# Two edits in a two-layer decoder kernel: the mLSTM gates loaded chunk by chunk, and the compressor's input kept in its own order

## The chip, the cores and the metric
The kernel runs on one core of a Trainium2 chip. The metric is the device time of one execution in microseconds (us); less is better. The inputs are fixed, all data is float32, and the whole program is one launch.

## The reference, cut to what matters
One inference step of a two-layer trunk, for a prompt of 1024 tokens and a sample group of 8 x 8 tokens. Layer 0 has mLSTM heads (4 heads, keys of 64, values of 128) beside gated DeltaNet heads. Layer 1 has NSA heads, one of whose branches attends to compressed blocks, beside FoX heads. The two places that the change touches compute this:

```python
# mLSTM, for each chunk of tokens, after the chunkwise recurrence gave num and den:
#   h = num / max(|den|, bound);  h = rmsnorm(h) * mi_norm;  out = h * sigmoid(output gate)
# NSA compression: overlapping blocks of 32 tokens, stride 16, of keys (kv = 0) and values (kv = 1):
#   unit  = the 16 tokens x 64 numbers of one stride, flattened
#   block = two units in a row + position embedding, flattened to 2048
#   out   = silu(block @ cmp_w1) @ cmp_w2          # 2048 -> 256 -> 64
```

## The kernel before, in words
The program is a row of stages. Each stage has its own instruction lists for TensorE (PE), ScalarE (ACT), VectorE (DVE), GpSimd (POOL) and the DMA queue of SyncE (SP). Each list runs in the order written. A wait in a list (`need`, `wait_ge`) holds up all that stands behind it in that list. At the end of a stage all engines meet at a barrier, so a stage lasts as long as its longest chain. A float32 matmul of the code is two matmul instructions in the trace (64 in the code of L2319 are 128 in the trace); data marked with `r32` is one pass.

**The stage `mlstm`.** The tokens are handled in nine chunks: the sample group (called NC, index k = 0), then the prompt chunks i = 0 to 7 of 128 tokens (index k = i + 1). For chunk i, PE prepares chunk i + 1 (`prepare`: row broadcasts, transposes, scores ST, L542 to L558), reads out chunk i (`read_out`, L580, L582), and updates the state (`update`, L592). DVE adds masks (`decay`, L752), multiplies weights, moves the numerator out of PSUM (`out`, L792 to L799, with a `tensor_scalar` at L795) and updates the state (L780). ACT takes exponentials (L648), and sums of squares of a chunk (L666).

The end of each chunk is done later, as a chain of steps for each index k: `scaled(k)` on DVE (L822) multiplies by a factor; `turn_back(k)` on PE (L612) transposes four heads into the one PSUM bank HT; `gated(k)` on DVE (L829) multiplies by the gate into Z; `high(k)` on ACT (L676) rounds; `low(k)` on POOL (L724) subtracts. `turn_back(k)` waits for `gated(k - 1)`, since there is one HT bank. The factors come from `factors(n)` on DVE (L805 to L815), for a batch of chunks at a time, with a square root on ACT (L671) in its middle. The square root needs another activation table than the exponential.

Before, there are three batches: k = 0 to 4 (factors at i = 3), k = 5, 6 (factors at i = 5), k = 7, 8 (factors behind the loop). The chunk ends are handled as this table says; 7 and 8 come behind the loop:

```python
    batches = (slice(0, 5), slice(5, 7), slice(7, 9))
    finished = {4: (0, 1), 5: (2, 3), 6: (4,), 7: (5, 6)}
```

The gates (sigmoid already taken, in DRAM as `G`) are loaded by one DMA (L503) for all tokens, and multiplied by mi_norm on POOL (L720, four instructions of 128 x 1092) before the first `low`.

**The stage `tables`.** Twelve groups of 256 tokens (four of the prompt, eight of the sample group's pages) come in through four slots (L2192, L2198). PE turns each (L2252) so that numbers lie in the partitions. ACT copies a group from PSUM into X with two instructions, one for keys and one for values (L2367). X has, in each partition, 8 runs (a = 0 to 7) of 386 numbers: run a holds the number of each unit n at place a. The compressor is the loop at L2319: 4 kinds (keys or values, two halves of the hidden size) of 16 matmuls, each with 385 moving columns, which lie side by side in X. Behind each kind DVE copies one column (L2422) and ACT applies silu (L2371). The last two columns hold the position embedding, loaded by four DMAs of ACT's queue (L2350).

**Elsewhere.** One line outside of both stages is used as a yardstick, at L1206 in the stage `delta`:

```python
            step("VT", A.activation(VT, V.rearrange("p s t -> p t s"), ACT.Copy))
```

It copies 128 x 1024 numbers from SBUF to SBUF. It writes them side by side and reads them with a step of 32 numbers. L398 copies as many from SBUF to SBUF, side by side on both sides; L404 half as many. In `stream`, L236 is the matmul with `r32` data.

Of the kernel before, what the change touches and what calls it, by code (L numbers as in the profile page):

```python
# [18 lines left out]
P = 128  # L19
# [420 lines left out]
def mlstm(pr, I, O, C, Z, GC, RT, G, gam, blocks, bufs, ps):  # L440
# [5 lines left out]
    num, gate = room([P, NC + 1, 4, P]), room([P, 4, TP])  # L446
# [5 lines left out]
    hs, junk = room([P, 2, 4, P]), room([P, P])  # L452
# [3 lines left out]
    batches = (slice(0, 5), slice(5, 7), slice(7, 9))  # L456
    finished = {4: (0, 1), 5: (2, 3), 6: (4,), 7: (5, 6)}
# [29 lines left out]
    with pr.stage("mlstm", steps=["pe", "act", "dve", "pool"], sems=["state", "blocks", "gam", "gate", "st"]) as (block, s):  # L487
# [3 lines left out]
        def _(sp):  # L491
# [11 lines left out]
            sp.dma_start(gate, G[0:4].rearrange("h p t -> p h t")).then_inc(s["gate"], 16)  # L503
            sp.wait_ge(dve_.sem, dve_.at(("Cb", NB - 1)))
            for x in range(2):
                sl = slice(64 * x, 64 * x + 64)
                for b in range(NB):
                    sp.dma_start(O["s_mlstm_c"][0, b].rearrange("(y x) d v -> x d y v", x=2)[x], Cb[sl, b, :, 0:P]).then_inc(s["st"], 16)
                for y in range(2):
                    sp.dma_start(O["s_mlstm_n"][0, :, 2 * y + x, :].rearrange("b (d o) -> d b o", o=1), Cb[sl, :, y, P:P + 1],  # L510
                                 allow_slow_non_contiguous=True).then_inc(s["st"], 16)
            sp.wait_ge(dve_.sem, dve_.at(("C", NC - 1)))
            for x in range(2):
                sl = slice(64 * x, 64 * x + 64)
                sp.dma_start(O["p_mlstm_c"][0, 0].rearrange("(y x) d v -> x d y v", x=2)[x], Cs[sl, NC % 2, :, 0:P]).then_inc(s["st"], 16)
                sp.dma_start(O["p_mlstm_n"][0, 0].rearrange("(y x) (d o) -> x d y o", x=2, o=1)[x], Cs[sl, NC % 2, :, P:P + 1],
                             allow_slow_non_contiguous=True).then_inc(s["st"], 16)
            sp.wait_ge(s["st"], 16 * 24)

        @block.tensor  # L520
        def _(pe):
# [97 lines left out]
            for i in range(NC):  # L619
# [8 lines left out]
                for k in finished.get(i, ()):  # L628
                    turn_back(k)
            for k in (7, 8):  # L630
                turn_back(k)

        @block.scalar
        def _(act):
# [34 lines left out]
            def root(n):  # L669
                need(dve_, ("mean", n))  # L670
                step(("root", n), A.activation(part[:, batches[n]], part[:, batches[n]], ACT.Sqrt))  # L671
# [8 lines left out]
            for i in range(NC):  # L680
# [5 lines left out]
                if i == 5:  # L686
                    root(1)
                for k in finished.get(i, ()):
                    high(k)
            root(2)  # L690
            for k in (7, 8):
                high(k)

        @block.gpsimd
        def _(pool):
# [22 lines left out]
            pool.wait_ge(s["gate"], 16)  # L718
            for h in hs4:
                step(("gate", h), E.tensor_tensor(gate[:, h], gate[:, h], gam[:, h:h + 1].broadcast_to([P, TP]), ALU.mult))  # L720
            for k in range(NC + 1):
                w = wide(order[k])
                need(act_, ("high", k))
                step(("low", k), E.tensor_tensor(r32(Z[:, 4:8, w]), Z[:, 4:8, w], r32(Z[:, 0:4, w]), ALU.subtract))  # L724

        @block.vector
        def _(dve):
# [73 lines left out]
            def factors(n):  # L801
                w = batches[n]
                need(act_, ("ssq", order[w.stop - 1]))
                need(dve_, ("bound", order[w.stop - 1]))
# [12 lines left out]
            def scaled(k):  # L817
# [3 lines left out]
                need(dve_, ("fac", 0 if k < 5 else 1 if k < 7 else 2))  # L821
                step(("hs", k), V.tensor_tensor(hs[0:r, k % 2], num[0:r, k], spread(fac[0:r, k], P), ALU.mult))  # L822

            def gated(k):
# [3 lines left out]
                need(pool_, ("gate", 3))  # L828
                step(("z", k), V.tensor_tensor(Z[:, 4:8, cols(i)], HT[:, :, 0:r], gate[:, :, cols(i)], ALU.mult))  # L829
# [5 lines left out]
            for i in range(NC):  # L835
# [14 lines left out]
                for k in finished.get(i, ()):  # L850
                    gated(k)
                    if k < 3:
                        scaled(k + 2)
                if i == 5:
                    factors(1)
                if i == 6:
                    scaled(5)
                    scaled(6)
            factors(2)
            scaled(7)  # L860
            scaled(8)
            for k in (7, 8):
                gated(k)

# [1291 lines left out]
def tables(pr, I, O, C, W, T, foxsel, w1, arena, ps):  # L2156
# [6 lines left out]
    X = [arena([P, 8, UNITS + 2]) for _ in range(2)]  # L2163
# [14 lines left out]
    with pr.stage("tables", steps=["pe", "act", "dve"],  # L2178
# [60 lines left out]
        def _(pe):  # L2239
# [71 lines left out]
            pe.wait_ge(s["w"], 16 * 8)  # L2311
# [4 lines left out]
            for kv, m in kinds:  # L2316
                hb = bank(ps, hidden_bank[(kv, m)])[:, 0:UNITS + 1]
                for a in range(16):
                    mm = pe.matmul(hb, w1[:, kv, a, P * m:P * (m + 1)], X[kv][:, a % 8, a // 8:a // 8 + UNITS + 1], start=(a == 0), stop=(a == 15))  # L2319
# [16 lines left out]
        def _(act):  # L2336
# [9 lines left out]
            for kv in range(2):  # L2346
                for x in range(2):
                    act.dma_start(w2[kv][:, :, 64 * x:64 * x + 64], I["nsa_cmp_w2"][0, kv].rearrange("(m q) d -> q m d", q=P)).then_inc(s["w"], 16)
                for x in range(2):
                    act.dma_start(X[kv][:, :, UNITS + x:UNITS + x + 1], I["nsa_cmp_pos"][0, kv].rearrange("(x a w o) d -> x (w d) a o", x=2, w=2, o=1)[x],  # L2350
                                  allow_slow_non_contiguous=True).then_inc(s["w"], 16)
# [6 lines left out]
            for u in range(NU):  # L2358
                need(pe_, ("X", u))
                for kv in range(2):  # L2360
                    src = bank(ps, u % 2)[:, 256 * kv:256 * kv + 256].rearrange("p (g n a) -> p g n a", g=2, a=8)
                    n0 = 16 * u if u < 4 else 128 + 32 * (u - 4)
                    to = X[kv][:, :, 0:128] if u < 4 else X[kv][:, :, n0:n0 + 32]
                    dst = to.rearrange("p a (g n) -> p g n a", g=2)
                    if u < 4:
                        dst = dst[:, :, n0:n0 + 16, :]
# [1440 lines left out]
```

## Time and profile before

| what | us |
|---|---|
| median of 3 runs | 3739.52 |
| lowest, highest run | 3734.91, 3739.58 |
| the profiled execution, its own time | 3739.52 |
| its span in the trace | 3737.4 |
| PE busy | 3411.3 (91% of the span) |
| stage `mlstm`, first to last instruction | 451.3 to 574.0 |
| stage `tables`, first to last instruction | 1979.8 to 2088.3 |
| of it, the matmuls of L2319 | 2037.6 to 2081.7 |

How to read it: the span runs from the first to the last instruction of the trace, and lies 2.1 us below the execution's own time. Busy shares are means over a program whose stages have different limits, so what a change is worth is read in its stage.

### The profile page before, as it was taken

The numbers are of one execution on the slowest core, as the hardware profiler recorded it, in microseconds if no ns is written. First come the engines' busy times: TensorE is split into PE (matmuls) and PEld (weight loads), VectorE is DVE, ScalarE is ACT, GpSimd is POOL, SyncE is SP. The second block draws the span as 40 slices with busy tenths as digits, with TensorE's granted clock in tenths as the row PEclk, the third lists the DMA queues.
The fourth block names the chain that finished last, engine by engine and source line by source line (L and its number), as shares of the span: only waits on it lengthen the run. The fifth ranks groups of instructions, "written<-read, shape, count | busy, mean of one in ns | idle before, by whom it ended". The sixth has DMA issues, their size and how long they took to land. (4 is left out here: it accounts for less than half of the span.)

```text
span 3737.4 us, 47454 instructions
## 1 busy us (share of the span) xinstructions
PE 3411.3 (91%) x20367; PEld 3195.1 (85%) x20367; DVE 1352.4 (36%) x1920; ACT 614.7 (16%) x1120; POOL 1204.8 (32%) x583
## 2 busy tenths in 40 slices
PE   6989898999999999989997796999778999999998
PEld 6989778889999999988795585788558999999998
DVE  4951145424323241431001354555325332323142
ACT  4310134321000000110001132233122100000012
POOL 4433212533444443424040120111003344444442
PEclk8999877899999999999997896999768999999999
DMA  4111221221111111123132322000222111111111
GB/s 129 46 35 47 86 36 42 61 99 34 46 46 46 41 45 46 52 87 117 45 90 65 74 42 58 7 7 7 73 68 93 40 46 46 41 45 46 46 46 59
DMA packets 298695, 204.12 MB, mean 55 GB/s; under 512 B 61377, under 2 KB 278803, under 8 KB 297944
## 3 DMA queue, kind: packets, MB, share of 16 engines
q1 hardware_dynamic: 292960, 200.66, 18.6%
q8 instruction: 161, 2.64, 0.3%
q10 hardware_dynamic: 5528, 0.45, 0.1%
q14 instruction: 46, 0.38, 0.0%
HBM read 158.88 MB, written 33.40 MB: 51 GB/s over the span
## 5 line engine op out<-in xcount | busy, mean ns | idle before, releaser
L236 PE MATMUL ps<-u_r,wslots_r 128*128 128x364 f32 x4608 | 772.5, 330 | 0.0
L236 PEld LDWEIGHTS ps<-u_r,wslots_r 128*128 128x128 f32 x4608 | 771.0, 189 | 0.0
L203 POOL TENSOR_TENSOR wslots_r<-rawm,sb_ones 128x1024 fp32r<-128x1024 f32 x133 | 322.9, 2428 | 910.2 <-PE ps L236 873.4
L236 PE MATMUL ps<-hn_r,wslots_r 128*128 128x364 f32 x2880 | 590.6, 331 | 13.1 <-POOLq L197 13.1
L236 PE MATMUL ps<-low_r,wslots_r 128*128 128x364 f32 x2688 | 544.2, 330 | 15.3 <-POOLq L197 15.0
L236 PEld LDWEIGHTS ps<-hn_r,wslots_r 128*128 128x128 f32 x2880 | 498.1, 190 | 13.6 <-POOLq L197 13.6
L236 PEld LDWEIGHTS ps<-low_r,wslots_r 128*128 128x128 f32 x2688 | 462.7, 189 | 15.9 <-POOLq L197 15.3
L205 POOL TENSOR_TENSOR wslots_r<-rawm,wslots_r 128x1024 fp32r<-128x1024 f32 x133 | 379.0, 2849 | 10.4
L1862 DVE TENSOR_TENSOR xT<-xT,ps 128x1092 f32<-128x1092 f32 x80 | 103.4, 1292 | 651.3 <-PE ps L236 651.3
L1584 PE MATMUL ps<-hn_r,wslots_r 128*128 128x364 f32 x1392 | 278.9, 334 | 17.9 <-POOLq L1554 9.2
L1584 PEld LDWEIGHTS ps<-hn_r,wslots_r 128*128 128x128 f32 x1392 | 240.4, 191 | 24.3 <-DVE Z L1814 10.0
L2999 PE MATMUL ps<-xT 128*128 128x128 f32 (+7 forms) x1184 | 170.2, 289 | 1.8 <-DVE xT L3200 0.9
L2999 PEld LDWEIGHTS ps<-xT 128*128 128x128 f32 (+7 forms) x1184 | 153.6, 200 | 18.2 <-issue 8.7
L1584 PE MATMUL ps<-xT_r,wslots_r 128*128 128x364 f32 x696 | 155.5, 332 | 0.0
L1559 POOL TENSOR_TENSOR wslots_r<-raw,sb_ones 128x1024 fp32r<-128x1024 f32 x28 | 69.7, 2491 | 227.9 <-PE ps L1584 206.0
L1903 ACT ACTIVATE u_r<-u 128x1092 fp32r<-128x1092 f32 x32 | 35.8, 1118 | 628.3 <-DVE u L1900 628.3
L1903 ACT ACTIVATE low_r<-hn 128x1092 fp32r<-128x1092 f32 x32 | 35.8, 1118 | 627.7 <-DVE hn L1900 627.7
L1584 PEld LDWEIGHTS ps<-xT_r,wslots_r 128*128 128x128 f32 x696 | 123.1, 191 | 0.0
L3083 ACT ACTIVATE xT<-ps 128x512 f32<-128x512 f32 (+5 forms) x148 | 85.3, 598 | 175.0 <-DVE ps L3179 117.0
L1897 DVE TENSOR_TENSOR hn<-ps,row 128x1092 f32<-128x1092 f32 x32 | 41.5, 1295 | 186.2 <-PE ps L236 170.6
L1897 DVE TENSOR_TENSOR u<-ps,row 128x1092 f32<-128x1092 f32 x32 | 41.4, 1295 | 175.9 <-PE ps L236 170.6
L236 PE MATMUL ps<-Z_r,wslots_r 128*128 128x364 f32 x576 | 98.9, 335 | 4.9 <-PEq L76 4.9
(612 smaller groups left out, 4738.5 us busy)
## 6 DMA issues: line engine op xcount, KB each, us to landing
rawm<-in_w_down SPq DMA_DIRECT2D x64, 512.0 KB, 3.6
rawm<-in_w_up SPq DMA_DIRECT2D x63, 512.0 KB, 4.0
raw<-in_w_in_even SPq DMA_DIRECT2D x28, 512.0 KB, 3.7
xT<-x_saved SPq DMA_DIRECT2D x2, 4368.0 KB
xT<-in_cache_fox_kv SPq DMA_DIRECT2D x16, 512.0 KB, 3.8
more_r<-more_r SPq DMA_DIRECT2D x28, 256.0 KB
panel_raw<-in_w_in_odd SPq DMA_DIRECT2D x6, 1024.0 KB, 5.3
x_saved<-Z SPq DMA_DIRECT2D x1, 4368.0 KB
```

What stands on the lines that cost most here:

```text
L203: nc.gpsimd.tensor_tensor(r32(half[0][:, g % 2]), raw[:, g % 2], one, ALU.mult).then_inc(s["high"], 1)
L205: nc.gpsimd.tensor_tensor(r32(half[1][:, g % 2]), raw[:, g % 2], r32(half[0][:, g % 2]), ALU.subtract) \
L236: mm = pe.matmul(view[n % 2][:, c, :], r32(half[a][:, n % 2, k, :]), r32(t["x"][b][:, k, CH * c:CH * (c + 1)]), start=(k == 0 and (a, b) = ...
L1559: G_.tensor_tensor(r32(half[0][:, g % 2]), raw[:, g % 2], one, ALU.mult).then_inc(s["high"], 1)
L1584: mm = pe.matmul(acc[:, c, :], r32(half[a][:, g % 2, k, :]), r32((hn, low)[b][:, k, CH * c:CH * (c + 1)]), start=(k == 0 and (a, b) == HAL ...
L1862: return e.tensor_tensor(v3(xT[:, n, :]), v3(xT[:, n, :]), acc, ALU.add)
L1897: return e.tensor_tensor(v3(u[1][:, n, :]), acc, v3(row), ALU.mult)
L1903: return e.activation(r32(u[0][:, n, :]), u[1][:, n, :], ACT.Copy)
L2999: mm = pe.matmul(out(u, kind)[:, h, :], prob[0:r, n % 3, P * h:P * (h + 1)], v, start=(n == branch_first[(u, kind)] and h == 0), stop=(n = ...
L3083: nc.scalar.activation(prob[0:r, n % 3, :], S(n)[0:r], ACT.Exp).then_inc(act_.sem, act_.mark(("exp", n)))
```

## The change
In `mlstm`, the gates are no longer loaded at once. A ring of two buffers holds the gates of a chunk. SP loads the gates of index k with `load_gate(k)`, which for k of 2 and more waits for `gated(k - 2)`. POOL multiplies them with `weigh(k)`, one instruction for each chunk; `weigh(k + 2)` stands right behind `low(k)` in POOL's list. In SP's list the loads 2 to 5 stand behind the stores of the sample states, and the loads 6 to 8 behind the stores of the prompt's state. There are two batches of factors (0 to 4, and 5 to 8) instead of three. Chunk ends 0 and 1 are handled at i = 4, then one at each of i = 5, 6, 7 (2, 3, 4), and four (5 to 8) behind the loop.

In `tables`, X keeps the order in which PSUM has the numbers: unit by unit, 8 numbers each. ACT's copy writes side by side. The matmul reads its 385 columns with a step of 8 numbers (32 bytes). The position embedding comes by one DMA for keys and one for values, instead of two each.

```diff
-    num, gate = room([P, NC + 1, 4, P]), room([P, 4, TP])
+    num = room([P, NC + 1, 4, P])
-    hs, junk = room([P, 2, 4, P]), room([P, P])
+    hs, gate, junk = room([P, 2, 4, P]), room([P, 2, 4, P]), room([P, P])
-    batches = (slice(0, 5), slice(5, 7), slice(7, 9))
-    finished = {4: (0, 1), 5: (2, 3), 6: (4,), 7: (5, 6)}
...
-            sp.dma_start(gate, G[0:4].rearrange("h p t -> p h t")).then_inc(s["gate"], 16)
+            def load_gate(k):
+                if k >= 2:
+                    sp.wait_ge(dve_.sem, dve_.at(("z", k - 2)))
+                i = order[k]
+                sp.dma_start(gate[:, k % 2, :, 0:token_rows(i)], G[0:4, :, cols(i)].rearrange("h p t -> p h t")).then_inc(s[f"gate{k % 2}"], 16)
+            load_gate(0)
+            load_gate(1)
             sp.wait_ge(dve_.sem, dve_.at(("Cb", NB - 1)))
...
+            for k in range(2, 6):
+                load_gate(k)
             sp.wait_ge(dve_.sem, dve_.at(("C", NC - 1)))
...
+            for k in range(6, NC + 1):
+                load_gate(k)
             sp.wait_ge(s["st"], 16 * 24)
...
-                for k in finished.get(i, ()):
-                    turn_back(k)
-            for k in (7, 8):
+                if i == 4:
+                    turn_back(0)
+                if i >= 4:
+                    turn_back(i - 3)
+            for k in range(5, NC + 1):
                 turn_back(k)
...
-                if i == 5:
-                    root(1)
-                for k in finished.get(i, ()):
-                    high(k)
-            root(2)
-            for k in (7, 8):
+                if i == 4:
+                    high(0)
+                if i >= 4:
+                    high(i - 3)
+            root(1)
+            for k in range(5, NC + 1):
                 high(k)
...
-            pool.wait_ge(s["gate"], 16)
-            for h in hs4:
-                step(("gate", h), E.tensor_tensor(gate[:, h], gate[:, h], gam[:, h:h + 1].broadcast_to([P, TP]), ALU.mult))
+            def weigh(k):
+                r = token_rows(order[k])
+                pool.wait_ge(s[f"gate{k % 2}"], 16 * (k // 2 + 1))
+                step(("gate", k), E.tensor_tensor(gate[:, k % 2, :, 0:r], gate[:, k % 2, :, 0:r], spread(gam[:, 0:4], r), ALU.mult))
+            weigh(0)
+            weigh(1)
             for k in range(NC + 1):
                 w = wide(order[k])
                 need(act_, ("high", k))
                 step(("low", k), E.tensor_tensor(r32(Z[:, 4:8, w]), Z[:, 4:8, w], r32(Z[:, 0:4, w]), ALU.subtract))
+                if k + 2 <= NC:
+                    weigh(k + 2)
...
-                need(pool_, ("gate", 3))
+                need(pool_, ("gate", k))
...
-                for k in finished.get(i, ()):
-                    gated(k)
-                    if k < 3:
-                        scaled(k + 2)
-                if i == 5:
-                    factors(1)
-                if i == 6:
-                    scaled(5)
-                    scaled(6)
-            factors(2)
-            scaled(7)
-            scaled(8)
-            for k in (7, 8):
+                if i == 4:
+                    gated(0)
+                    scaled(2)
+                if i >= 4:
+                    gated(i - 3)
+                    if i < 6:
+                        scaled(i - 1)
+            factors(1)
+            scaled(5)
+            scaled(6)
+            for k in range(5, NC + 1):
                 gated(k)
+                if k + 2 <= NC:
+                    scaled(k + 2)
...
-    X = [arena([P, 8, UNITS + 2]) for _ in range(2)]
+    X = [arena([P, 8 * (UNITS + 2)]) for _ in range(2)]
...
-                    mm = pe.matmul(hb, w1[:, kv, a, P * m:P * (m + 1)], X[kv][:, a % 8, a // 8:a // 8 + UNITS + 1], start=(a == 0), stop=(a == 15))
+                    c0 = 8 * (a // 8) + a % 8
+                    mm = pe.matmul(hb, w1[:, kv, a, P * m:P * (m + 1)], X[kv][:, c0:c0 + 8 * UNITS + 1:8], start=(a == 0), stop=(a == 15))
...
-                for x in range(2):
-                    act.dma_start(X[kv][:, :, UNITS + x:UNITS + x + 1], I["nsa_cmp_pos"][0, kv].rearrange("(x a w o) d -> x (w d) a o", x=2, w=2, o=1)[x],
-                                  allow_slow_non_contiguous=True).then_inc(s["w"], 16)
+                act.dma_start(X[kv][:, 8 * UNITS:8 * UNITS + 16], I["nsa_cmp_pos"][0, kv].rearrange("(a w) d -> (w d) a", w=2),
+                              allow_slow_non_contiguous=True).then_inc(s["w"], 16)
...
-                    src = bank(ps, u % 2)[:, 256 * kv:256 * kv + 256].rearrange("p (g n a) -> p g n a", g=2, a=8)
-                    n0 = 16 * u if u < 4 else 128 + 32 * (u - 4)
-                    to = X[kv][:, :, 0:128] if u < 4 else X[kv][:, :, n0:n0 + 32]
-                    dst = to.rearrange("p a (g n) -> p g n a", g=2)
+                    src = bank(ps, u % 2)[:, 256 * kv:256 * kv + 256].rearrange("p (g n) -> p g n", g=2)
                     if u < 4:
-                        dst = dst[:, :, n0:n0 + 16, :]
+                        dst = X[kv][:, 0:1024].rearrange("p (g n) -> p g n", g=2)[:, :, P * u:P * (u + 1)]
+                    else:
+                        dst = X[kv][:, 1024 + 256 * (u - 4):1024 + 256 * (u - 3)].rearrange("p (g n) -> p g n", g=2)
                     ins = A.activation(dst, src, ACT.Copy)
```

## Rows read from the trace of the kernel before

**Rows 1.** Stretches: us, busy PE, PEld, DVE, ACT, POOL; clock, DMA share, GB/s.
```profile
562.00:575.00 13.00, 3.29 (x12) 2.15 (x12) 5.02 (x12) 4.38 (x8) 5.05 (x4) 0.50 0.06 10
...
2037.50:2082.00 44.50, 44.44 (x133) 25.76 (x134) 0.63 (x4) 2.92 (x5) 0.00 (x0) 0.94 0.01 1
```
**Rows 2.** Timeline of the end of `tables`: start, us, engine, line, operation, idle before.
```profile
2036.27 1.08 ACT L2367 ACTIVATE xT<-ps 128x256 f32<-128x256 f32 x2 [2.81 <-PE ps L2252]
2037.56 44.19 PE L2319 MATMUL ps<-xT,cmp_w 128*128 128x385 f32 x128 [1.34 <-ACT xT L2367]
...
2050.69 0.16 DVE L2422 COPY more<-ps 128x1 f32<-128x1 f32 x1 [28.20 <-PE ps L2319]
...
2061.05 0.16 DVE L2422 COPY more<-ps 128x1 f32<-128x1 f32 x1 [10.20 <-PE ps L2319]
```
**Rows 3.** Timeline of L236, matmuls with one-pass data.
```profile
1971.01 1.15 PE L236 MATMUL ps<-hn_r,wslots_r 128*128 128x364 f32 x6
1972.00 0.66 PE L236 MATMUL ps<-xT_r,wslots_r 128*128 128x364 f32 x3
1972.50 1.17 PE L236 MATMUL ps<-hn_r,wslots_r 128*128 128x364 f32 x6
```
**Rows 4.** ACT's groups by shape: count, busy us, mean ns, idle before.
```profile
L2367 ACT ACTIVATE xT<-ps 128x256 f32<-128x256 f32 x24 | 12.9, 651 | 34.3 <-PE ps L2252 34.3
...
L404 ACT ACTIVATE hn_r<-xT 128x512 fp32r<-128x512 f32 x16 | 9.1, 623 | 0.0
L398 ACT ACTIVATE Z<-Z 128x1024 f32<-128x1024 f32 x8 | 8.4, 1049 | 2.0 <-DMA Z<-in_x_prompt 2.0
...
L657 ACT ACTIVATE xT<-ps 128x512 f32<-128x512 f32 x8 | 4.7, 584 | 0.0
...
L653 ACT ACTIVATE hn<-ps 128x256 f32<-128x256 f32 x8 | 3.0, 369 | 0.4
```
**Rows 5.** The instruction of L1206: ns min, median, max, start.
```profile
L1206 ACT ACTIVATE hn<-hn x1: 1942/1942/1942, 653.7 to 653.7; 128x1024 f32<-128x1024 f32 x1
```
**Rows 6.** The matmuls of L531, moving operand read with a step of 8.
```profile
L531 PE MATMUL ps<-RT,sb_sel x8: 253/254/255, 451.5 to 452.1; 128*64 128x8 f32 x8
```
**Rows 7.** Timeline of `mlstm` at i = 5.
```profile
542.30 0.66 PE L612 MATMUL ps<-sb_ident,wslots 128*128 128x128 f32 x4
...
544.32 1.09 PE L612 MATMUL ps<-sb_ident,wslots 128*128 128x128 f32 x4 [1.36 <-DVE Z L829]
...
547.44 0.68 DVE L752 TENSOR_TENSOR hn<-ps,sb_maskP 128x512 f32<-128x512 f32 x1
```
**Rows 8.** Timeline of `mlstm` at the end of i = 3.
```profile
510.11 8.40 POOL L720 TENSOR_TENSOR hn<-hn,gam 128x1092 f32<-128x1092 f32 x4
...
517.03 1.51 DVE L795 TENSOR_SCALAR wslots<-wslots 128x4 f32<-128x4 f32 x1
...
518.87 1.28 ACT L671 ACT_TABLE_LOAD   x1
...
520.84 0.22 ACT L671 ACTIVATE wslots<-wslots 128x20 f32<-128x20 f32 x1 [0.68 <-DVE wslots L811]
```
**Rows 9.** Timeline of the tail of `mlstm`.
```profile
560.83 1.11 PE L612 MATMUL ps<-sb_ident,wslots 128*128 128x128 f32 x4
...
561.98 0.69 DVE L829 TENSOR_TENSOR Z<-ps,hn 128x512 f32<-128x512 f32 x1 [0.35 <-PE ps L612]
...
563.94 0.69 DVE L829 TENSOR_TENSOR Z<-ps,hn 128x512 f32<-128x512 f32 x1 [1.27 <-PE ps L612]
...
567.36 1.29 DVE L822 TENSOR_TENSOR wslots<-xT,wslots 128x512 f32<-128x512 f32 x2
...
571.22 0.69 DVE L829 TENSOR_TENSOR Z<-ps,hn 128x512 f32<-128x512 f32 x1 [1.27 <-PE ps L612]
...
572.72 1.26 POOL L724 TENSOR_TENSOR Z_r<-Z,Z_r 128x512 fp32r<-128x512 f32 x1 [0.70 <-ACT Z_r L676]
```
**Rows 10.** DMAs of L968 (gates, in `delta`): count, size, us from issue to landing.
```profile
wslots<-gate_tiles SPq DMA_DIRECT2D x8, 256.0 KB, 2.9
```

More of the change, by code:

```diff
@@ L486, in spread @@
         return v.rearrange("p (h o) -> p h o", o=1).broadcast_to([v.shape[0], 4, n])
-    with pr.stage("mlstm", steps=["pe", "act", "dve", "pool"], sems=["state", "blocks", "gam", "gate", "st"]) as (block, s):
+    with pr.stage("mlstm", steps=["pe", "act", "dve", "pool"], sems=["state", "blocks", "gam", "gate0", "gate1", "st"]) as (block, s):
         pe_, act_, dve_, pool_ = s["pe"], s["act"], s["dve"], s["pool"]
@@ L670, in root @@
                 need(dve_, ("mean", n))
-                step(("root", n), A.activation(part[:, batches[n]], part[:, batches[n]], ACT.Sqrt))
+                step(("root", n), A.activation(part[:, 5 * n:5 * n + 5 - n], part[:, 5 * n:5 * n + 5 - n], ACT.Sqrt))
             def high(k):
@@ L801, in factors @@
             def factors(n):
-                w = batches[n]
-                need(act_, ("ssq", order[w.stop - 1]))
-                need(dve_, ("bound", order[w.stop - 1]))
+                w = slice(5 * n, 5 * n + 5 - n)
+                need(act_, ("ssq", 3 + 4 * n))
+                need(dve_, ("bound", 3 + 4 * n))
                 step(("rden", n), V.reciprocal(den[:, w], den[:, w]))
@@ L820, in scaled @@
                     need(pe_, ("HT", k - 2))
-                need(dve_, ("fac", 0 if k < 5 else 1 if k < 7 else 2))
+                need(dve_, ("fac", 0 if k < 5 else 1))
                 step(("hs", k), V.tensor_tensor(hs[0:r, k % 2], num[0:r, k], spread(fac[0:r, k], P), ALU.mult))
@@ L827, in gated @@
                 need(pe_, ("HT", k))
-                need(pool_, ("gate", 3))
-                step(("z", k), V.tensor_tensor(Z[:, 4:8, cols(i)], HT[:, :, 0:r], gate[:, :, cols(i)], ALU.mult))
+                need(pool_, ("gate", k))
+                step(("z", k), V.tensor_tensor(Z[:, 4:8, cols(i)], HT[:, :, 0:r], gate[:, k % 2, :, 0:r], ALU.mult))
             decay(NC)
@@ L2310, in _ @@
                 turned(u)
-            pe.wait_ge(s["w"], 16 * 8)
+            pe.wait_ge(s["w"], 16 * 6)
             need(act_, ("X", NU - 2))
```

## The prediction

> **What bounds the kernel now.** I read the page first. PE is busy for 91% of the span, but a mean over stages says nothing on this change, so I went to the two stages by stretches, then to their timelines, and last to groups by shape for the prices.
>
> The stretch of L2319 is the plainest part [rows 1]: of 44.5 us PE is busy for 44.44, at a granted clock of 0.94, and the other engines hardly work. The timeline says the same [rows 2]: the matmuls start 0.2 us after ACT's last copy into X ends, and DVE waits 10.20 us for each kind. Nothing here hides PE. What a matmul of L2319 gains or loses is gained or lost by the kernel, 128 times.
>
> The tail of `mlstm` is the opposite case [rows 1]: in 13 us no engine works for more than 5.05 us, and the clock is at the lower level, 1.2 GHz. A chain of short steps from engine to engine sets it, and its last link is POOL's L724, ending at 572.72 + 1.26 = 573.98 [rows 9].
>
> **The matmuls of L2319.** The count of instructions, columns and weight loads stays. Only the reading of the moving operand changes: 385 numbers with a step of 32 bytes, instead of side by side. Before, a kind of 32 instructions takes 2061.05 - 2050.69 = 10.36 us [rows 2], or 324 ns each. That is 0.84 ns for a column.
>
> No row shows a long float32 operand read with such a step. L531 reads 8 columns with exactly this step [rows 6], but 8 columns are too few: 254 ns is nearly all latency. So I bound the cost from both sides.
>
> The bound from below is nothing. With one-pass data L236 issues 9 matmuls of 364 columns in 1972.50 - 1971.01 = 1.49 us [rows 3], 0.45 ns a column including overhead. The float32 matmul asks for a column only every 0.84 ns, so PE's reading has nearly half of its speed to spare. If a jump to a new place costs one such slot, and each column is fetched once, it is free. No reason here gives a gain.
>
> The nearest rows that do read or write with a step are ACT's. L398 and L404 copy side by side from SBUF to SBUF: (1049 - 623) / 512 = 0.83 ns a number, and 197 ns fixed [rows 4]. L1206 copies 1024 numbers that it reads with a step of 128 bytes, in 1942 ns [rows 5]: (1942 - 197) / 1024 = 1.70 ns a number, 2.05 times as much. The writing side shows it too: L2367 writes 256 numbers, each to another run of X, in 651 ns, where L653 writes 256 side by side in 369 [rows 4]. With L657's 584 ns for 512 the slope of that plain form is 0.84 ns and its fixed part 154 ns; L2367 then takes (651 - 154) / 256 = 1.94 ns a number. Reading and writing each cost about twice per number once every number lies apart, and the contiguous 0.83 ns of ACT is the very rate at which PE's float32 columns come. I take the reading row, 1.70 ns: 385 x 1.70 = 656 ns a matmul, 332 more than 324. The first 8 of the 128 ran at 645 ns, at the lower clock: (2050.69 - 2037.56 - 32 x 0.324) / 0.321 = 8.6 of them [rows 2]. They already take what the read would. So 120 x 332 = 39.8 us, and I take +40. By the writing row, 385 x 1.94 = 747 ns: 120 x 423 + 8 x 102 = +51.6, the upper bound.
>
> The Trainium skill (SBUF — State Buffer, § SBUF: two separate sides) says that SBUF has lines of 16 bytes, that at least two hits on a line are wanted to hide its access, and that an access that crosses to a new line pays. That speaks against this change, since a step of 32 bytes puts each column in a line of its own. ACT's rows agree with it; whether a float32 matmul, at half the rate of one-pass data, has the time to absorb it, the page does not say. Read as "half of full rate" it would give +0, read as "twice the own time" 128 x 324 = +41.5.
>
> **ACT's copies into X.** 24 of them fall from 651 to about 369 ns [rows 4]. Only the last pair lies on the path (PE starts behind it [rows 2]); the others run while PE waits for pages. The pair takes 1.08 us; side by side about 0.6. That is -0.5. The position DMAs are two fewer in ACT's queue; L2319 waits for them, but they stand at the head of ACT's list, ahead of all twelve groups, so they cost 0. If that cover were gone they would cost one DMA, 2.9 us [rows 10].
>
> **`mlstm`, the middle.** At i = 5 PE does one turn instead of two. Before, the second started at 544.32 and held its 0.9 us, so the preparation of chunk 7 began at about 545.2 instead of 542.30 + 0.66 = 542.96 [rows 7]. Between it and D(7) at 547.44 DVE also had `gated(3)` and the middle batch of factors, with two table loads of ACT. All of that goes; D(7), and behind it the read-out, comes about 2.4 us earlier. At i = 3 POOL's L720 runs until 518.51, and DVE's L795 takes 1.51 us for 128 x 4 numbers; it ends at 518.54, with POOL [rows 8]. A DVE copy as small takes 0.16 [rows 2]. Two short products (L724's price, 1.26 each [rows 9]) end before 513, so this stall goes. The square root behind it started at 520.84, and can't before its table load ends at 518.87 + 1.28 = 520.15 [rows 8], so of 1.35 us only about 0.6 reach `factors(0)`. Middle: -3.0.
>
> The Trainium skill (SBUF — State Buffer, § Who interferes with whom) has the reason for that stall: GpSimd and a VectorE `tensor_scalar` in a 2-port mode lock the same pair of ports for a whole instruction. Rows 8 agree, with 1.51 us. By this rule a later `weigh` can hold up L795 likewise, by up to 1.3 us.
>
> **`mlstm`, the tail.** Before, from the first turn at 560.83 to the end at 573.98: 13.15 us [rows 9], with two ends, the factors, and two ends. After, from the turn of k = 4: its gate starts 1.15 later; `scaled(5)` 567.36 - 563.94 = 3.42 later, at 4.57; the turn of 5 behind its half of L822's 1.29, at 5.3; `gated(5)` at 6.5 to 7.2. Two ends are 1.96 apart (563.94 - 561.98), so without the ring `gated(8)` would start at 12.4 and, with 573.98 - 571.22 = 2.76 behind it, the end is at 15.1: +2.0. But `load_gate(7)` waits for `gated(5)`. It lands 2.9 us later [rows 10], at 10.1, and POOL's product of 1.26 [rows 9] ends at 11.4, so `gated(7)` is at 11.4 and not at 10.4. In POOL's list `low(6)`, `weigh(8)`, `low(7)` and `low(8)` follow, each 1.26: 12.7, 14.0, 15.3, and 16.6. The tail is 16.6 - 13.15 = 3.5 longer. The earlier loads (2 to 6) land before their chunk ends. `mlstm` as a whole: +0.5, and from -1.0 (no ring delay) to +4 (a blocked L795 of 1.3, and two landings 1 us later each).
>
> **The sum.** Against the profiled execution's 3739.5, which is also the median: +40 - 0.5 + 0.5 = 3779.5.
>
> **The rivals.**
> 1. The step is free. PE takes a float32 column every 0.84 ns but can take one every 0.45 [rows 3]. Then the time is 3739.5 + 0.0, from 3738 to 3743: no change. It speaks for this that nothing but ACT shows the price; against it, that ACT is no slower side by side (0.83) and still doubles. It decides from the point where a fetch of a lone number takes less than 0.84 ns. The change is then an exchange of 2.4 us in the middle for 3.5 in the tail.
> 2. The step costs more than once. If two passes of a float32 column fetch it twice, at 1.70 ns each, a matmul takes 385 x 3.40 = 1309 ns, and the kernel 3739.5 + 128 x 0.985 = 3866. Only the factor of two between L236 and L2319 speaks for it.
> 3. A part of the price: a fetch of 0.9 to 1.3 ns gives 23 to 180 ns a matmul, +3 to +22.
> 4. Faster: the ring hides wholly, the step is free, and the saved table loads also keep PE at 2.4 GHz in the tail, which now runs at 1.2 [rows 1]. All 3.29 us of PE's busy time there halved would be -1.6, with -1.0 and -0.5 about -3: 3736. To fall by 0.2% something must happen that I don't see.
>
> **How the numbers follow.** 0.2% is 7.5 us, about what a measurement of this kernel can tell from no change. Chances: forecast (+25 to +55) 0.50; the free step 0.33; more than +60 0.06; +8 to +25 0.06; faster 0.05. So slower 0.62, same 0.33, faster 0.05. The range from 3737 to 3795 holds the free case, the part price and the forecast up to its bound of +51.6 with +4 for `mlstm`; the likeliest case's own range is 3765 to 3795.
>
> **What would show it.** In the changed profile, the columns copied at L2422 stand 32 x 0.656 = 21 us apart if I am right, 10.4 if the step is free, 42 if it is paid twice; the stage `tables` is 40 us longer. The copies of L2367 take about 370 ns. In `mlstm`, there are two loads of the square root's table instead of three; no DVE instruction of 128 x 4 takes 1.5 us at i = 3; the turn of k = 7 or its gate waits for POOL; the stage is within 4 us of before. The prediction is wrong if PE's read at a step behaves otherwise than ACT's: that one term carries it.

## The result, and the profile after

| | before | after |
|---|---|---|
| median, us | 3739.55 (4 runs) | 3796.01 (4 runs) |
| lowest, highest | 3734.91, 3740.94 | 3793.30, 3803.72 |
| span of the profiled execution | 3737.4 | 3794.4 |

The change costs 56.5 us by these medians. The ratio is 1.0163, with a 95% interval of 1.0146 to 1.0180, which is some 61 us: twelve executions of the changed kernel were timed in all, and their median is 3797.31. The forecast was 3779.5, and its range ended at 3795. One of the eight executions of experiment 2 below took 7136.86 us, in a slow state, and counts in the median given there but not in the ratio.

The lines of the kernel move by 2 to 17 with the change: L2336 is the matmul that was L2319, L2437 the copy that was L2422, L731 and L737 are POOL's product and `low`, L844 is `gated`, L505 the gate load.

**The compressor.** First the timeline of the changed kernel at the end of `tables`, of PE, ACT and DVE, against [rows 2].

```profile
2049.22 0.66 ACT L2382 ACTIVATE xT<-ps 128x256 f32<-128x256 f32 x2 [1.95 <-PE ps L2268]
...
2050.09 88.92 PE L2336 MATMUL ps<-xT,cmp_w 128*128 128x385 f32 x128 [0.92 <-ACT xT L2382]
...
2072.62 0.16 DVE L2437 COPY more<-ps 128x1 f32<-128x1 f32 x1 [36.12 <-PE ps L2336]
2094.76 0.16 DVE L2437 COPY more<-ps 128x1 f32<-128x1 f32 x1 [21.98 <-PE ps L2336]
```

The columns stand 22.14 us apart instead of 10.36. That is 692 ns an instruction and 1.80 ns a column, where the forecast had 21 us, 656 and 1.70. The whole group takes 88.92 us instead of 44.19, +44.7. PE waits for nothing in it. This is the stretch of these matmuls (columns as in [rows 1]); the granted clock of 0.97 says that PE ran at the upper level, 2.4 GHz, for nearly all of it:

```profile
2050.00:2139.10 89.10, 89.01 (x130) 27.58 (x131) 0.52 (x4) 2.93 (x4) 0.00 (x0) 0.97 0.01 2
```

So one can't see from the busy share that PE is fed too slowly. The weight loads (PEld) show it: they are busy for 27.58 of 89.10 us, where it was 25.76 of 44.50 [rows 1]. ACT's last pair takes 0.66 us instead of 1.08, but from the start of `tables` to the first of these matmuls it is 57.8 us in both traces (2037.56 - 1979.76 and 2050.09 - 1992.28).

**The gates.** Here is the surprise. `mlstm` is 15.5 us longer: from the first DMA of the stage to the first of the next it took 575.23 - 451.25 = 123.98 us, and takes 591.39 - 451.88 = 139.51. The first fence is SP's timeline of the changed kernel (DMA issues; the time behind the start is that of issuing, waits within a group included), the second POOL's with one row of DVE.

```profile
531.81 2.92 SPq L514 DMA_DIRECT2D out_s_mlstm_n<-xT  x2
...
534.78 26.69 SPq L505 DMA_DIRECT2D hn<-gate_tiles  x4
...
570.76 0.61 SPq L522 DMA_DIRECT2D out_p_mlstm_n<-xT  x1
571.41 12.12 SPq L505 DMA_DIRECT2D hn<-gate_tiles  x3
```

```profile
547.62 1.04 POOL L731 TENSOR_TENSOR hn<-hn,gam 128x512 f32<-128x512 f32 x1 [13.46 <-DMA hn<-gate_tiles]
...
564.44 1.04 POOL L731 TENSOR_TENSOR hn<-hn,gam 128x512 f32<-128x512 f32 x1 [1.30 <-DMA hn<-gate_tiles]
...
570.63 1.26 POOL L737 TENSOR_TENSOR Z_r<-Z,Z_r 128x512 fp32r<-128x512 f32 x1 [5.15 <-ACT Z_r L686]
581.32 1.04 POOL L731 TENSOR_TENSOR hn<-hn,gam 128x512 f32<-128x512 f32 x1 [9.43 <-DMA hn<-gate_tiles]
...
589.21 1.26 POOL L737 TENSOR_TENSOR Z_r<-Z,Z_r 128x512 fp32r<-128x512 f32 x1 [0.26 <-ACT Z_r L686]
...
582.46 0.69 DVE L844 TENSOR_TENSOR Z<-ps,hn 128x512 f32<-128x512 f32 x1 [6.66 <-POOL hn L731]
```

The load of k = 2 is issued at 534.78 and its product starts at 547.62, 12.8 us later. That of k = 6 is issued at 571.41 and used at 581.32, 9.9 later. The load between them, k = 5 (product at 564.44), made POOL wait for only 1.30 us. The same transfer in `delta` takes 2.9 [rows 10]. Both late loads stand right behind stores of `out_s_mlstm_n` or `out_p_mlstm_n`, whose packets are 4 bytes. In the tail DVE waits 6.66 us for POOL, and the turns, the `low` steps and all that stands behind them wait too.

**Where the 57.0 us of span are**, by the start of each stage in the two traces: 0.6 before `mlstm`, 15.5 in it, -1.9 in `delta`, -1.7 from there to `tables`, 44.75 in `tables`, and -0.3 behind it. The 1.9 of `delta` go along with a higher clock. In its first 50 us, before and after, PE gets through 405 matmuls instead of 392, at a granted clock of 0.91 instead of 0.88:

```profile
575.20:625.20 50.00, 48.23 (x392) 45.83 (x392) 21.79 (x57) 31.57 (x96) 13.07 (x12) 0.88 0.26 65
591.40:641.40 50.00, 48.27 (x405) 45.77 (x405) 21.77 (x57) 31.58 (x96) 13.08 (x12) 0.91 0.26 65
```

### The profile page after: what moved, and what is told of

Its sections match the earlier page's. It is cut to its first block and busy times, and to the rows that moved or that the text cites. A ratio compares the mean times of both kernels' runs of the same rounds, so it can differ in the third digit from the quotient of the medians.

```text
span 3794.4 us, 47463 instructions
## 1 busy us (share of the span) xinstructions
PE 3455.1 (91%) x20367; PEld 3194.5 (84%) x20367; DVE 1353.7 (36%) x1914; ACT 606.9 (16%) x1117; POOL 1204.5 (32%) x588
## 5 line engine op out<-in xcount | busy, mean ns | idle before, releaser
L236 PE MATMUL ps<-u_r,wslots_r 128*128 128x364 f32 x4608 | 772.3, 330 | 0.0
L236 PEld LDWEIGHTS ps<-u_r,wslots_r 128*128 128x128 f32 x4608 | 770.8, 189 | 0.0
L236 PE MATMUL ps<-hn_r,wslots_r 128*128 128x364 f32 x2880 | 589.7, 331 | 13.2 <-POOLq L197 13.2
L236 PE MATMUL ps<-low_r,wslots_r 128*128 128x364 f32 x2688 | 543.8, 330 | 15.9 <-POOLq L197 15.0
L236 PEld LDWEIGHTS ps<-hn_r,wslots_r 128*128 128x128 f32 x2880 | 497.1, 189 | 13.6 <-POOLq L197 13.6
L236 PEld LDWEIGHTS ps<-low_r,wslots_r 128*128 128x128 f32 x2688 | 462.2, 189 | 16.5 <-POOLq L197 15.3
L236 PE MATMUL ps<-Z_r,wslots_r 128*128 128x364 f32 x576 | 97.8, 332 | 4.7 <-PEq L76 4.7
```

The lines of the kernel that those rows point to most:

```text
L236: mm = pe.matmul(view[n % 2][:, c, :], r32(half[a][:, n % 2, k, :]), r32(t["x"][b][:, k, CH * c:CH * (c + 1)]), start=(k == 0 and (a, b) = ...
```

## The experiments

In their expectations, "theory A", "B" and "rival" are those that stood at the time. Diffs are against the kernel before, or against "the ring alone", which is the kernel before with the change's `mlstm`.

**1 and 2. The two edits apart.** One kernel has the change of `tables` alone, the other that of `mlstm` alone.

> The kernel before with the change of `tables` alone: X in plain order, the matmuls of L2319 read it with a step of 8 numbers. Theory (the step is paid in full, at 1.80 ns a column, and the rest of the change is nothing here): 128 x (693 - 324) ns is 47.2 us, less 8 or 9 that ran at the lower clock before and less 0.4 of ACT's last pair, so +44.7 us, 3784. The columns copied at L2422 stand 22.2 us apart. Rival (the 44.7 us of the changed kernel came in part from its other edits, by the clock or a shifted DMA): +35 or less.

> The kernel before with the change of `mlstm` alone (two gate buffers loaded by chunk, two batches of factors). Theory (the two edits are apart and add up): `mlstm` is 15.5 us longer, `delta` and the stages behind give 3 back, so +12 us, 3751 to 3753; the loads of k = 2 and k = 6 land 12.7 and 9.9 us after their issue. Rival (the chip's state in that one profile of the changed kernel made them late): landings of 3 us, as for the gates of `delta`, and +1 to +4 us.

`tables` alone: 3782.14, ratio 1.0120 (1.0105 to 1.0135), +43.2 us, columns 22.14 us apart. The ring alone: 3751.48, ratio 1.0036 (1.0024 to 1.0048), +12.5. Together 55.7, against 56.5 measured. So the two edits hardly touch each other. The late loads are there again in the ring alone (product of k = 2 at 545.49, of k = 6 at 578.79, 9.5 us behind its issue at 569.29).

**3. The schedule without the ring.** The whole gate load and POOL's four products are kept; only batches and turns are the change's.

> The kernel before with its whole gate load and its four products on POOL, and only the schedule of the change: two batches of factors, one chunk finished in a turn, k = 5 to 8 behind the loop. Theory (the loss of `mlstm` is the ring's): the middle comes 2.4 us earlier, the tail is 2.0 us longer, so within 1.5 us of before. Rival (the schedule itself costs: four chunks behind the loop where there were two, at the lower clock): +5 us or more of the 12 to 15.

```diff
-    batches = (slice(0, 5), slice(5, 7), slice(7, 9))
-    finished = {4: (0, 1), 5: (2, 3), 6: (4,), 7: (5, 6)}
+    batches = (slice(0, 5), slice(5, 9))
+    finished = {4: (0, 1), 5: (2,), 6: (3,), 7: (4,)}
```

3736.39, ratio 0.9995 (0.9987 to 1.0004): no change. The stage takes 122.84 us, 1.1 less than before. Up to the tail (which starts with the first turn at i = 7, of k = 5 before and of k = 4 with two batches) it is 3.2 shorter, and the tail is 2.0 longer, as the forecast had it without the ring. The loss is the ring's.

**4. The loads on another queue.** ACT issues them, each behind its copy `high(k)`, which waits for the same `gated(k)`.

> The change of `mlstm` alone, but the gate loads of k = 2 to 8 are issued by ACT, each behind its copy of chunk k - 2, and no longer by SP behind the state stores. Theory A (the loads are late because they stand in SP's queue behind the stores): they land about 3 us after their issue, POOL waits for no gate, and of the 12 us at least 9 go: +0 to +4 us. Theory B (the stores keep the DMA engines themselves busy, whoever issues): the loads of k = 2 and k = 6 still land 8 to 12 us after their issue, and the time stays at +9 to +13.

```diff
                 step(("high", k), A.activation(r32(Z[:, 0:4, wide(i)]), Z[:, 4:8, wide(i)], ACT.Copy))
+                if k + 2 <= NC:
+                    i = order[k + 2]
+                    act.dma_start(gate[:, k % 2, :, 0:token_rows(i)], G[0:4, :, cols(i)].rearrange("h p t -> p h t")).then_inc(s[f"gate{k % 2}"], 16)
```

3745.94, ratio 1.0018 (1.0009 to 1.0026), +7.0. That lies between the two theories, so the trace decides. ACT's and POOL's timelines of this kernel:

```profile
565.46 0.37 ACTq L685 DMA_DIRECT2D hn<-gate_tiles  x1
...
574.81 1.04 POOL L730 TENSOR_TENSOR hn<-hn,gam 128x512 f32<-128x512 f32 x1 [7.33 <-DMA hn<-gate_tiles]
```

The load of k = 6 is issued earlier, while SP still issues the p stores (564.41 to 566.35), and is used 9.35 us later. The load of k = 2 is issued at 532.06 and used at 543.67, 11.6 later. What was gained is the earlier issue. The landing is as late from another queue, so it is not SP's queue that holds the load. The Trainium skill (DMA: Bandwidth & Descriptors, § Issuing engines are not separate DMA queues) says that transfers of all issuing engines run on the same 16 DMA engines and interleave; the trace agrees, with 9.35 us against 9.5.

**5. No 4-byte stores.** The ring alone, without the stores of the state's n: `s_mlstm_n` (4 stores, 2,048 numbers) and `p_mlstm_n` (2 stores, 256 numbers) aren't written.

> The change of `mlstm` alone (L505 on SP, as in the change), and the six stores of single numbers (state n, 4 bytes each) are left out: s_mlstm_n and p_mlstm_n aren't written. Behind the second pair of p stores the load of k = 6 took 9.5 us, while in the kernel with the batches alone the same four p stores, with no load behind them, left the DMA engines idle within 1.7 us of the last issue. Theory A (the 4-byte writes are what the loads wait for): the loads of k = 2 and k = 6 land 3 to 4 us after their issue and the time falls from +12.5 to +1 to +5 us. Theory B (the 64 KB stores of c, or store and load together, are enough): the loads still take 7 us or more, and at least +8 us is left. Theory C (the load is slow by itself in this place, whatever stands beside it): nothing changes, +11 to +13.

```diff
-                for y in range(2):
-                    sp.dma_start(O["s_mlstm_n"][0, :, 2 * y + x, :].rearrange("b (d o) -> d b o", o=1), Cb[sl, :, y, P:P + 1],
-                                 allow_slow_non_contiguous=True).then_inc(s["st"], 16)
...
-                sp.dma_start(O["p_mlstm_n"][0, 0].rearrange("(y x) (d o) -> x d y o", x=2, o=1)[x], Cs[sl, NC % 2, :, P:P + 1],
-                             allow_slow_non_contiguous=True).then_inc(s["st"], 16)
```

3735.64, ratio 0.9997 (0.9987 to 1.0006): the 12.5 us are gone, which is more than theory A expected (+1 to +5). The median is 2.8 below that of before, but the interval holds 1. In the profile, `mlstm` takes 122.98 us, 1.0 less than before, and `delta` is 3.9 shorter, which these loads don't explain (see Left open). The timelines of SP and POOL of this kernel, where the same loads stand behind the same stores of c:

```profile
518.59 10.42 SPq L512 DMA_DIRECT2D out_s_mlstm_c<-xT  x16
531.20 18.77 SPq L505 DMA_DIRECT2D hn<-gate_tiles  x4
556.94 1.26 SPq L518 DMA_DIRECT2D out_p_mlstm_c<-xT  x2
558.24 7.58 SPq L505 DMA_DIRECT2D hn<-gate_tiles  x3
```

```profile
534.07 1.04 POOL L726 TENSOR_TENSOR hn<-hn,gam 128x512 f32<-128x512 f32 x1 [1.27 <-DMA hn<-gate_tiles]
...
561.28 1.05 POOL L726 TENSOR_TENSOR hn<-hn,gam 128x512 f32<-128x512 f32 x1 [1.26 <-DMA hn<-gate_tiles]
```

From issue to product it is now 2.9 and 3.0 us. The 128 KB of c that are issued right before the load of k = 6 cost it nothing (the 1 MB before k = 2 had been out for 0.7 us when that load was issued); the 9 KB of single numbers cost the loads 6.5 to 10 us.

**6 and 7. The 4-byte stores moved, not left out.** In one kernel all six stand behind the last gate load, in the other only the two of `p_mlstm_n`.

> The change of `mlstm` alone, with all six stores of 4-byte numbers moved to the end of SP's list, behind the last gate load. Theory A: the loads land in 3 to 4 us as without these stores, but 2,304 packets of 4 bytes then stand at the end, where the stage waits for them; with some 6 us for them (530 to 536 us in the traces, where they have the queue to themselves) the time is +4 to +10 us. Theory B: the loads still take 7 us or more and the time is above +12.

> The change of `mlstm` alone, with only the two stores of p_mlstm_n (128 packets of 4 bytes each) moved behind the last gate load; those of s_mlstm_n stay where they were. Theory A (each load is held up by the 4-byte writes just ahead of it): the load of k = 2 still takes 11 us, that of k = 6 lands in 3 us, the stage is 6 to 7 us shorter than with them in place, +5 to +7 us instead of +12.6. Rival (256 small packets are too few; the 2,048 of the sample states were what spoiled both): the load of k = 6 still takes 7 us or more, +10 to +13.

```diff
             for k in range(6, NC + 1):
                 load_gate(k)
+            for x in range(2):
+                sl = slice(64 * x, 64 * x + 64)
+                sp.dma_start(O["p_mlstm_n"][0, 0].rearrange("(y x) (d o) -> x d y o", x=2, o=1)[x], Cs[sl, NC % 2, :, P:P + 1],
+                             allow_slow_non_contiguous=True).then_inc(s["st"], 16)
```

All six: 3744.04, ratio 1.0022 (1.0013 to 1.0031), +5.6. The loads land in time (POOL waits at most 1.55 us for one), its last `low` starts at 572.40, but the next stage starts only at 584.14: now the end of the stage waits for the stores. It comes 13.5 us after the last of them was issued (570.02 + 0.64). The time is within theory A's +4 to +10, though the stores take twice its 6 us. Only `p_mlstm_n`: 3744.14, ratio 1.0014 (1.0005 to 1.0023), +6.4. POOL's timeline of this kernel separates the two causes:

```profile
545.67 1.04 POOL L733 TENSOR_TENSOR hn<-hn,gam 128x512 f32<-128x512 f32 x1 [11.45 <-DMA hn<-gate_tiles]
...
571.23 1.04 POOL L733 TENSOR_TENSOR hn<-hn,gam 128x512 f32<-128x512 f32 x1 [1.29 <-DMA hn<-gate_tiles]
```

The sample states' n still holds up k = 2; k = 6 lands 3.1 us after its issue at 568.16. The stage takes 132.06 us, 5.6 less than the ring alone. So 256 packets of 4 bytes are enough to hold a load of 256 KB by 6.5 us.

**8 to 11. What the matmul's read costs.** Four kernels multiply other numbers than the reference's. Experiments 8 and 10 are float32, with a step of 4 and of 2 numbers. Experiments 9 and 11 are one-pass (`r32`), with a step of 8 and of 1, both operands from X, which ACT writes rounded, and 384 columns. The lines below are those of 8 and, last, of 9.

> The kernel before, with L2319 reading X with a step of 4 numbers (16 bytes) instead of 1; other numbers than the reference's are multiplied. Theory (what costs is that every column lies in another 16-byte piece): the matmul takes as long as with 32 bytes, 693 ns, L2422 apart by 22.2 us, +44 us. Rival (the price grows with the distance, or comes from both halves of a 32-byte piece): 500 ns or less, under +22 us.

> The kernel before with X in the changed order, but the matmuls are one-pass (rounded float32, both operands from X, 384 columns, other numbers than the reference's) and read with a step of 8 numbers. Theory (float32 fetches each column once and waits 1.80 ns for it): one-pass data waits just as long, 384 x 1.80 = 690 ns a matmul, so L2422 stands 22 us apart, +44 us. Rival (float32 goes through its columns twice and pays 0.90 ns at each fetch): 384 x 0.90 = 346 ns, 11 us apart, about +1 us.

> The kernel before, with L2319 reading X with a step of 2 numbers (8 bytes), so that two columns still lie in each piece of 16 bytes; other numbers than the reference's are multiplied. With 16 bytes the instruction took 678 ns (1.76 ns a column), side by side 324 (0.84). Theory (one fetch of a 16-byte piece takes 0.85 to 0.9 ns, twice for each float32 column, and serves all columns in it): 0.88 ns a column, hidden behind the 0.84 of the arithmetic, so 324 to 345 ns, L2422 10.4 to 11 us apart, +0 to +3 us. Rival (a step of any size leaves the quick way of reading): 650 ns or more, +42 us.

> As the one-pass kernel with a step of 8, but with a step of 1 (rounded float32, both operands from X, 384 columns, other numbers than the reference's). With a step of 8 an instruction took 325 ns, 0.85 ns a column. Theory (a lone column costs a fetch of 0.85 ns, which one-pass data pays once and float32 twice): side by side it runs at the rate of its 384 columns, 160 to 175 ns, 2.6 to 2.8 us a kind, 10 us less than with the step of 8, 3708. Rival (325 ns was the one-pass matmul's own time with its weights loaded from X, and the step cost nothing there): 325 ns again, 3718.

```diff
-                    mm = pe.matmul(hb, w1[:, kv, a, P * m:P * (m + 1)], X[kv][:, a % 8, a // 8:a // 8 + UNITS + 1], start=(a == 0), stop=(a == 15))
+                    mm = pe.matmul(hb, w1[:, kv, a, P * m:P * (m + 1)], X[kv].rearrange("p a n -> p (a n)")[:, a % 8:a % 8 + 4 * UNITS + 1:4], start=(a == 0), stop=(a == 15))
...
+                    mm = pe.matmul(hb[:, 0:UNITS], r32(X[kv][:, P * a:P * (a + 1)]), r32(X[kv][:, c0:c0 + 8 * (UNITS - 1) + 1:8]), start=(a == 0), stop=(a == 15))
```

Each was run once, with a profile: 3780.70 us (8), 3717.94 (9), 3737.36 (10) and 3709.28 (11). With one run each, the times of the whole kernel only back up the traces. These are the copies that close two kinds, from DVE's timeline of each, in the order 8, 9, 10, 11; a kind has 32 instructions in float32 and 16 in one pass. The granted clock is 1.00 between the two copies of each kernel, and so it was before.

```profile
2081.39 0.16 DVE L2422 COPY more<-ps 128x1 f32<-128x1 f32 x1 [21.56 <-PE ps L2319]
2103.08 0.16 DVE L2422 COPY more<-ps 128x1 f32<-128x1 f32 x1 [21.53 <-PE ps L2319]
```

```profile
2047.52 0.16 DVE L2421 COPY more<-ps 128x1 f32<-128x1 f32 x1 [5.04 <-PE ps L2320]
2052.72 0.16 DVE L2421 COPY more<-ps 128x1 f32<-128x1 f32 x1 [5.04 <-PE ps L2320]
```

```profile
2059.38 0.16 DVE L2422 COPY more<-ps 128x1 f32<-128x1 f32 x1 [10.71 <-PE ps L2319]
2070.24 0.16 DVE L2422 COPY more<-ps 128x1 f32<-128x1 f32 x1 [10.70 <-PE ps L2319]
```

```profile
2038.93 0.16 DVE L2421 COPY more<-ps 128x1 f32<-128x1 f32 x1 [2.62 <-PE ps L2320]
2041.73 0.16 DVE L2421 COPY more<-ps 128x1 f32<-128x1 f32 x1 [2.64 <-PE ps L2320]
```

The expectation of experiment 9 counted 32 instructions a kind in one pass too, so its totals are too high; the time of one instruction is what tells. It was 325 ns: the theory's 690 fell, and the rival's 346 (0.90 ns at each fetch) was near. With steps of 2 and 1 the theory of then held (324 to 345 and 160 to 175 ns), its rivals fell. Divided by 32 or 16 instructions, and by their columns:

| step of the read | float32, ns (ns a column) | one-pass, ns (ns a column) |
|---|---|---|
| 1 | 324 (0.84) | 175 (0.46) |
| 2 (8 bytes) | 339 (0.88) | |
| 4 (16 bytes) | 678 (1.76) | |
| 8 (32 bytes) | 692 (1.80) | 325 (0.85) |

Three things stand in it. The jump lies between 8 and 16 bytes: two columns to a piece of 16 bytes are nearly free (15 ns), one costs all. From 16 to 32 bytes the distance hardly matters (14 ns). And a lone column costs one-pass data 0.85 ns, not 1.8. The float32 instruction takes 2.1 times as long on the same read, as if it fetched each column twice. In both kinds of data the price is about a doubling of the time side by side, 1.86 and 2.14 times. The Trainium skill (SBUF — State Buffer, § SBUF: two separate sides) wants two hits on a line of 16 bytes; the trace agrees, with 339 against 678 ns.

**12. The schedule with POOL's products by chunk, and no DMA in the loop.**

> The kernel before with its whole gate load, the two batches of the change, and POOL's product by chunk (two ahead of the loop, then one behind each chunk's `low`), so that no DMA lies in the loop. Theory (the ring cost only through its loads): no 1.5 us of L795 at i = 3, 0.6 us less than the kernel with the batches alone, whose stage was 1.1 us shorter than before; -1 to -3 us. Rival (a product in the loop blocks a small operation of VectorE, or stands between two `low` of the tail): +1 to +3.

```diff
-            for h in hs4:
-                step(("gate", h), E.tensor_tensor(gate[:, h], gate[:, h], gam[:, h:h + 1].broadcast_to([P, TP]), ALU.mult))
+            def weigh(k):
+                w = cols(order[k])
+                step(("gate", k), E.tensor_tensor(gate[:, :, w], gate[:, :, w], spread(gam[:, 0:4], token_rows(order[k])), ALU.mult))
+            weigh(0)
+            weigh(1)
```

3735.12, ratio 0.9994 (0.9985 to 1.0003). The interval holds 1, so it is not shown to be faster than before. Its stage takes 122.60 us, 1.4 less than before, and DVE's `tensor_scalar` at i = 3 takes 0.16 us (1.51 in experiment 3, where POOL's four long products are kept). It is the shortest `mlstm` of all these kernels.

## Why the prediction was wrong

**The steps in `tables` held; one term was 4.7 us too small.** The read lies in full on PE's path, and 120 x (692 - 324) is 44.2 of the 44.7. ACT's pair is 0.4 shorter, near the forecast's 0.5, but the stage shows nothing of it. "385 x 1.70 = 656 ns a matmul" was measured at 692, so +40 became +44.7 in the trace (+43.2 in the time for this edit alone). The row was a good guide in size and a poor one in kind. ACT's 1.70 ns is the time of one number on ACT; PE's 1.80 is, by experiments 8 to 11, some 0.85 ns for a fetch, twice for float32. That one of 1.70 and two of 0.85 come to the same is luck. The argument of rival 1, that PE "can take one every 0.45", was right only for columns side by side. Rival 2 had the two fetches right and their price, 1.70 each, twice too high. The bound from below set one fetch against 0.84 ns a column; one fetch of 0.85 would nearly have fitted, two don't. That float32 fetches twice is inferred from the two data types, and 28 and 42 ns of its 678 and 692 (2 x 325 = 650) stay unexplained.

**The step that failed is the ring.** "The earlier loads (2 to 6) land before their chunk ends", and "It lands 2.9 us later [rows 10]" was the price of a load. Rows 10 are loads with nothing small ahead of them. The text of the change said that loads 2 to 5 stand behind the sample states' stores and 6 to 8 behind the prompt's. The prediction has no term for what the stores ahead of a load are made of. The runs showed 12.8 and 9.9 us, and 2.9 and 3.0 once the stores of 4-byte numbers are gone. `mlstm` came to +15.5 and not +0.5, outside of its own bound of +4. The profile of before had a sign of it. The same pairs of small stores have no load behind them there, but the second pair took SP 4.72 us to issue instead of 1.28, and around 533 the DMA engines count as busy (a share of 1.35) while they move 13 GB/s (columns as in [rows 1]):

```profile
525.27 1.28 SPq L510 DMA_DIRECT2D out_s_mlstm_n<-xT  x2
...
531.82 4.72 SPq L510 DMA_DIRECT2D out_s_mlstm_n<-xT  x2
...
532.00:534.00 2.00, 1.39 (x8) 1.25 (x7) 1.33 (x5) 1.30 (x7) 0.50 (x1) 0.50 1.35 13
```

The span came out at +57.0 against a forecast of +40: 15.0 of the error lie in `mlstm`, 5.2 in `tables` (44.75 against 39.5), and the other stages gave 3.3 back, which the forecast didn't have.

**The rest of `mlstm` held, where the loads are not late.** In experiment 5 the tail's first turn starts at 556.11, 4.1 us nearer to the start of the stage than before (forecast 3.0), and the last `low` ends 572.72 - 556.11 = 16.6 us later (forecast 16.6). With the late loads these two parts are +6.5 and +9.3 (forecast -3.0 and +3.5). The changed kernel loads the square root's table twice instead of three times, and L810, which was L795, takes 0.16 us and not 1.51.

**The range** ended at 3795.0 and the median is 3796.01. Its upper end was the sum of the bounds of known rows; no row stood for a transfer behind small stores, so the end was too near.

**Left open.** Whether the 4-byte stores hold the load in the DMA engines or in what lies behind them. Alone, the four p stores leave the engines idle soon (experiment 3, with no load behind them; the columns are those of [rows 1], the last two are the DMA share and GB/s):

```profile
559.00:561.00 2.00, 0.00 (x0) 0.00 (x0) 0.55 (x4) 1.97 (x3) 1.26 (x1) 0.50 0.33 66
561.00:563.00 2.00, 0.59 (x3) 0.60 (x4) 1.72 (x4) 0.06 (x1) 0.00 (x0) 0.50 0.03 0
```

With the load behind them (experiment 2) the engines count as busy and move little:

```profile
570.00:572.00 2.00, 0.77 (x4) 0.71 (x4) 1.64 (x4) 0.00 (x0) 0.00 (x0) 0.50 0.62 10
572.00:574.00 2.00, 1.12 (x6) 0.71 (x4) 1.29 (x2) 0.63 (x1) 0.00 (x0) 0.50 0.40 38
```

Experiment 6 points behind the engines, but for the end of a stage and not for a load. SP waits there for nothing but its stores, the last of which was issued by 570.66. The last `low` is over at 573.66 and the next stage starts at 584.14 (0.9 us behind the last `low` in experiment 5, which has no such stores), yet in the 10 us between no DMA engine has a packet:

```profile
571.00:573.00 2.00, 0.00 (x0) 0.00 (x0) 0.59 (x1) 0.63 (x1) 1.75 (x2) 0.50 0.28 0
574.00:584.00 10.00, 0.00 (x0) 0.00 (x0) 0.00 (x0) 0.00 (x0) 0.00 (x0) 0.50 0.00 0
```

The Trainium skill (DMA: Bandwidth & Descriptors, § Specifications) says that transfers of less than 512 bytes are read, modified and written back. No run here shows whether that is what a following load waits for.

Why `delta` is shorter with the ring wasn't tried. From stage start to stage start it takes 202.65 us before and 200.73 after, and 200.48, 201.43, 198.73, 198.70 and 198.79 in experiments 2, 4, 5, 6 and 7, which have the ring. Without it, in experiments 3 and 12, it takes 202.57 and 202.24, though these too have 0.91 in the first 50 us. The late loads aren't needed for it: experiment 5 has none.

## What to carry to other kernels

Before a DMA is moved in a queue, look at what is ahead of it by packet size, not by bytes: 2,304 numbers of 4 bytes cost more than 1.1 MB of states, and another queue only brings the earlier issue. A load that a chain waits for belongs ahead of such stores, but the stores then need work behind them to hide under: moved to the end of this stage, they still cost 5.6 us. For a matmul's moving operand, keep at least two columns in each 16 bytes; a layout that saves a copy off the critical path isn't worth one that PE reads with a wider step. And price such a read by the data type: 385 columns cost float32 368 ns more, and 384 cost one-pass data 150.

## What the runs showed of the hardware that was not expected

- A load of 256 KB right behind 256 stores of 4 bytes lands after 9.5 to 9.9 us instead of 3.0, and behind 2,048 of them (the last 1,024 right ahead of it) after 11.5 to 12.8. It does so from ACT's queue too (9.35 and 11.6 us).
- Six such stores at the end of a stage hold its end: 13.5 us from the last issue to the next stage, in the last 10 of which no DMA engine is busy.
- PE's float32 read at a step: nearly free at 8 bytes (0.88 against 0.84 ns a column), twice the time at 16 (1.76), hardly more at 32 (1.80). One-pass data pays 0.85 against 0.46.
- A PE that is starved by its own reads looks busy: 89.01 of 89.10 us, at a granted clock of 0.97.
